# One shared table set for exponentials and logarithms, a first-block activation rounded straight from PSUM, and zero matmuls ahead of the norms

## What is computed

```
rms_norm(x, w) = x * rsqrt(mean(x*x) + 1e-6) * w
# block 1, two layers
h = rms_norm(x, pre_mix_norm[l])
proj = h @ w_in[l]            # queries, keys, values of four kinds of heads
a = neighbourhood attention; b = differential attention, then
    b = rms_norm(b, diff_subln[l]) * (1 - lambda_init)       # over 64 values of a head
c = grouped attention with normed and rotated q, k; d = latent attention
x = x + rms_norm(concat(a, b, c, d) @ w_o[l], post_mix_norm[l])
h = rms_norm(x, pre_ffn_norm[l])
x = x + rms_norm((silu(gate) * up) @ ffn_w_down[l], post_ffn_norm[l])   # gate, up = h @ ffn_w_gate_up
# block 2, four layers: mixers swa, gla, fox, swa
h = modulate(rmsnorm(x, gain), shift, scale);  x = x + g1 * mixer(h)
h = modulate(rmsnorm(x, gain), shift, scale);  x = x + g2 * swiglu(h)
# gla: log_alpha = log_sigmoid(z) / 16        fox: log_f = log_sigmoid(z + b)
```

## Time and profile before

| | |
|---|---|
| median of 3 runs | 1946.23 us (1945.25 to 1946.54) |
| the profiled execution's own time | 1951.02 us |
| its span in the trace | 1949.2 us |
| PE busy | 1883.7 us, 97% of the span, 13470 matmuls |
| PE weight loads busy | 1730.1 us, 89% |
| DVE busy | 1343.0 us, 69% |
| ACT busy | 995.4 us, 51% |
| ACT table loads in the program | 38 |
| chain that ended last, by engine | PE 81%, DVE 9%, ACT 4% of the span |

### The profile page before, as it was taken

How to read it: one execution, slowest core, us unless ns; L and a number is a source line. 1 busy time by engine, 2 the same in 40 slices (tenths; PEclk the granted TensorE clock), 3 DMA queues, 4 the chain that set the end, 5 groups by cost and what they waited for, 6 DMA issues and landing times.

```text
span 1949.2 us, 34518 instructions
## 1 busy us (share of the span) xinstructions
PE 1883.7 (97%) x13470; PEld 1730.1 (89%) x13470; DVE 1343.0 (69%) x2141; ACT 995.4 (51%) x1534; POOL 68.5 (4%) x82
## 2 busy tenths in 40 slices
PE   8999999999999999999999999998999999999998
PEld 7978999898899987899989799998989998979997
DVE  5757888675788876788878578885555555665555
ACT  7755333765533466633374453346655335655333
POOL 3002000000000000000000000003300000000000
PEclk9999999999999999999999999999999999999999
DMA  8527988532788842588853368874335554325552
GB/s 288 191 90 238 359 311 311 185 130 89 286 316 314 310 149 94 212 323 311 314 193 130 132 247 322 313 292 171 141 114 200 183 185 171 111 85 179 188 194 86
DMA packets 60355, 412.22 MB, mean 211 GB/s; under 512 B 8592, under 2 KB 8784, under 8 KB 11616
## 3 DMA queue, kind: packets, MB, share of 16 engines
q1 hardware_dynamic: 55728, 401.33, 55.7%
q0 software_dynamic: 4528, 9.56, 1.8%
HBM read 409.71 MB, written 3.16 MB: 212 GB/s over the span
## 4 chain that ended last, share of the span: by engine, by line
PE 81%; DVE 9%; ACT 4%; DVEq 2%; issue 2%; ACTq 1%; DMA 0%; SPq 0%
PE psu L502 33%; PE psy L661 16%; PE psy L564 6%; PE psy L610 5%; PE psy L556 4%; PE psm L736 3%; PE psu L519 3%; PE psu L721 2%; DVE wlo L855 2%; PE psy L632 2%; PE psy L543 1%; PE pso L707 1%; DVE ada_raw L1017 1%; DVE x L1084 1%; ACT whi L846 1%
## 5 line engine op out<-in xcount | busy, mean ns | idle before, releaser
L846 ACT CAST whi<-raw 128x2048 fp32r<-128x2048 f32 (+1 forms) x281 | 536.2, 1908 | 624.6 <-PE psu L502 424.3
L855 DVE TENSOR_TENSOR wlo<-raw,whi 128x2048 fp32r<-128x2048 f32 (+5 forms) x296 | 645.4, 2181 | 276.4 <-ACT whi L846 275.0
L502 PE MATMUL psu<-hhi,whi 128*128 128x256 f32 x1920 | 537.0, 280 | 0.0
L502 PE MATMUL psu<-hlo,whi 128*128 128x256 f32 x1920 | 535.9, 279 | 0.0
L502 PE MATMUL psu<-hhi,wlo 128*128 128x256 f32 x1920 | 535.8, 279 | 0.0
L502 PEld LDWEIGHTS psu<-hhi,whi 128*128 128x128 f32 x1920 | 360.8, 188 | 3.0
L502 PEld LDWEIGHTS psu<-hlo,whi 128*128 128x128 f32 x1920 | 360.8, 188 | 2.4
L502 PEld LDWEIGHTS psu<-hhi,wlo 128*128 128x128 f32 x1920 | 360.8, 188 | 0.0
L1017 DVE CUSTOM_DVE_ANT_0 ada_raw<-ada_raw,cvec 128x1024 f32<-128x1024 f32 x192 | 227.0, 1219 | 1.3 <-DMA ada_raw<-ada 1.2
L661 PE MATMUL psy<-whi,ahi 128*128 128x512 f32 x528 | 210.5, 399 | 1.0 <-DVE alo L1036 0.9
L661 PE MATMUL psy<-wlo,ahi 128*128 128x512 f32 x528 | 208.0, 394 | 0.0
(11 more groups left out here) (342 smaller groups left out, 3055.2 us busy)
## 6 DMA issues: line engine op xcount, KB each, us to landing
raw<-wts SPq DMA_DIRECT2D x280, 1024.0 KB, 4.8
ada_raw<-ada SPq DMA_DIRECT2D x96, 1024.0 KB, 4.8
dense_bias<-rel_bias POOLq DMA_DIRECT2D x32, 64.0 KB, 12.5
nab<-dense_bias SPq DMA_DIRECT2D x2, 1024.0 KB, 7.6
ada_raw<-fox_rows POOLq DMA_DIRECT2D x4, 512.0 KB, 6.8
cb<-cst POOLq DMA_DIRECT2D x1, 1408.0 KB, 8.5
cb<-cst SPq DMA_DIRECT2D x1, 1056.0 KB, 10.6
x<-x_in SPq DMA_DIRECT2D x2, 512.0 KB, 4.7
```

What stands on the lines that cost most here:

```text
L502: last = mm(psu[:, bank, cc * SEQ:(cc + 1) * SEQ], a[:, cols], h[:, kt, :], start=(kt == 0 and j == 0), stop=(kt == KT - 1 and j == 2))
L846: nc.scalar.copy(whi[:, part_of(c), 0:n], raw[:, slot_of(c), 0:n]).then_inc(hi_done, 1)
L855: last = nc.vector.tensor_tensor(wlo[:, part_of(c), cols], raw[:, slot_of(c), cols], whi[:, part_of(c), cols].bitcast(f32), ALU.subtract)
```

## The change

Four things are changed; the order of everything else stays.

1. In block one, `act_norm1` rounds from PSUM straight into `hhi`, two blocks at a time, and `dve_split1` takes the same PSUM value, multiplies it by the gain and subtracts `hhi`. The copy through `hw` is gone. Block two keeps the old way.
2. `pe_norm` starts 14, 14, 12, 14 and 6 zero matmuls (bf16, 128 x 512, into `psu[:, 1]`, which nothing reads) at m = 0 to 4, ahead of its wait for the first `xn_ready`.
3. In `pe_norm`, 4 blocks of the first token tile (2 at m = 0) stand ahead of the second tile's wait instead of 6, and the rest is put behind pairs of the second tile. This holds for all twelve norms.
4. `act_logs` loads a set that has both exponential and logarithm. In block one's slot 22 the root and reciprocal become exp(-0.5 ln(v)). Table loads fall from 38 to 30: by two in each layer of block one, two in gla and two in fox.

```diff
-                    pe.wait_ge(hhi_done, 8 * q + 4)
+                    pe.wait_ge(h_ready if q < 2 * DEPTH1 else hhi_done, 8 * q + 4)
...
-        def pe_norm(pe, m, q):
+        def pe_norm(pe, m, q, idle=0, ahead=4):
...
+            for _ in range(idle):
+                mm(fold(psu[:, 1], 4, P), zeros[:], zeros[:].unsqueeze(1).to_broadcast([P, 4, P]), start=True, stop=True)
             pe.wait_ge(xn_ready, NT * m + 1)
-            for kt in range(6):
+            for kt in range(ahead):
                 turned(kt, 0)
             pe.wait_ge(xn_ready, NT * m + 2)
             for kt in range(KT):
-                if kt >= 6:
-                    turned(kt, 0)
                 turned(kt, 1).then_inc(tr_done, 1)
+                if kt % 2 == 1:
+                    for k in range(ahead + kt - 1, min(ahead + kt + 1, KT)):
+                        turned(k, 0)
...
+        def act_logs():
+
+            nc.scalar.preload_act_table_set("natural_log_exp_and_others")
...
+        def act_norm1(act, q, gain, between=None):
+
+            for ks in PAIRS:
+                act.wait_ge(tr_done, 8 * q + ks[-1] + 1)
+                for k in ks:
+                    nc.scalar.activation(hhi[:, k], ps8[:, k], ACT.Identity, scale=gain[:, k:k + 1], bias=zcol[:]).then_inc(hhi_done, 1)
+                if between is not None:
+                    between(act, ks)
+
+        def dve_split1(dve, q, l, gain, between=None):
+
+            dve.wait_ge(pcol_loaded, 16 * (l + 1))
+            for ks in PAIRS:
+                dve.wait_ge(hhi_done, 8 * q + ks[-1] + 1)
+                for k in ks:
+                    nc.vector.scalar_tensor_tensor(out=hlo[:, k], in0=ps8[:, k], scalar=gain[:, k:k + 1], in1=hhi[:, k].bitcast(f32),
+                                                   op0=ALU.mult, op1=ALU.subtract).then_inc(h_ready, 1)
...
                 if h == 22:
                     act.wait_ge(sub_sum, l + 1)
-                    nc.scalar.activation(gs[:, 1, 0:8], gs[:, 0, 0:8], ACT.Sqrt, bias=epsc[:], scale=1.0 / HD).then_inc(sub_std, 1)
-                    act_table(ACT.Exp)
+                    nc.scalar.activation(gs[:, 1, 0:8], gs[:, 0, 0:8], ACT.Ln, bias=epsc[:], scale=1.0 / HD)
+                    nc.scalar.drain()
+                    nc.scalar.activation(gs[:, 2, 0:8], gs[:, 1, 0:8], ACT.Exp, scale=-0.5).then_inc(sub_std, 1)
...
                 dve.wait_ge(sub_std, l + 1)
-                nc.vector.reciprocal(gs[:, 2, 0:8], gs[:, 1, 0:8])
-                nc.vector.drain()
...
             items = heads_fox(b0)
+            act_logs()
             for h in range(FOX.slots):
...
                     nc.scalar.activation(f_l, f_l, ACT.Ln, bias=1.0).then_inc(fox_l, 1)
-                    act_table(ACT.Exp)
...
-                pe_norm(pe, 2 * l, 2 * l)
+                pe_norm(pe, 2 * l, 2 * l, 14 if l == 0 else 12, 2 if l == 0 else 4)
                 pe_mix1(pe, l)
-                pe_norm(pe, 2 * l + 1, 2 * l + 1)
+                pe_norm(pe, 2 * l + 1, 2 * l + 1, 14)
...
-                pe_norm(pe, 2 * g, 2 * g)
+                pe_norm(pe, 2 * g, 2 * g, 6 if n == 0 else 0)
```

More of the change, by code:

```diff
@@ L873, in build @@
         CHUNKS = ((0,), (1,), (2, 3), (4, 5), (6, 7))
+        PAIRS = ((0, 1), (2, 3), (4, 5), (6, 7))
         def act_sums(act, m):
@@ L893, in act_sums, with act_norm @@
                 last.then_inc(std_ready, 1)
-        def act_norm(act, q, scale, bias, between=None):
+        def act_norm1(act, q, gain, between=None):
[12 more added lines that the diff above has]
+                                                   op0=ALU.mult, op1=ALU.subtract).then_inc(h_ready, 1)
+                if between is not None:
+                    between(dve, ks)
+        def act_norm(act, q, scale, bias):
             for ks in CHUNKS:
@@ L899, in act_norm @@
                     nc.scalar.activation(hw[:, k], ps8[:, k], ACT.Identity, scale=scale[:, k:k + 1],
-                                         bias=zcol[:] if bias is None else bias[:, k:k + 1])
+                                         bias=bias[:, k:k + 1])
                 nc.scalar.drain()
                 nc.scalar.copy(hhi[:, ks[0]:ks[-1] + 1], hw[:, ks[0]:ks[-1] + 1]).then_inc(hhi_done, len(ks))
-                if between is not None:
-                    between(act, ks)
         def opening_split(act, ks):
-            if ks == (1,):
+            if ks == (0, 1):
                 act.wait_ge(raw_loaded[0], 16)
@@ L912, in opening_split, with dve_split @@
                 act_hi(act, 0, 1, first=True)
-        def dve_split(dve, q, between=None):
+        def dve_split(dve, q):
             for ks in CHUNKS:
@@ L919, in dve_split @@
                 nc.vector.tensor_tensor(hlo[:, ks_], hw[:, ks_], hhi[:, ks_].bitcast(f32), ALU.subtract).then_inc(h_ready, len(ks))
-                if between is not None:
-                    between(dve, ks)
         def opening_rest(dve, ks):
-            if ks == (1,):
+            if ks == (0, 1):
                 dve.wait_ge(hi_done, 1)
@@ L2000, in _ @@
             act.wait_ge(pcol_loaded, 16)
-            act_norm(act, 0, pcol[:, 0, 0:8], None, opening_split)
+            act_norm1(act, 0, pcol[:, 0, 0:8], opening_split)
             act_hi(act, 0, 2, first=True)
@@ L2049, in _ @@
                     dve_root_scales(dve, 2 * l, l, 1)
-                    dve_split(dve, 2 * l)
+                    dve_split1(dve, 2 * l, l, pcol[:, l, 0:8])
                     dve_lo(dve, l, 2)
@@ L2054, in _ @@
                 dve_root_scales(dve, 2 * l + 1, l, C1_FFN + 1)
-                dve_split(dve, 2 * l + 1)
+                dve_split1(dve, 2 * l + 1, l, pcol[:, l, 8:16])
                 dve_lo(dve, l, C1_FFN + 2)
```

6 lines of the change are left out of this document (3 added, 3 removed).

## The result

The changed kernel takes **1938.86 us** (median of 6 runs, 1938.36 to 1941.81) against 1946.38 us for the kernel before (6 runs): a ratio of 0.9963, 95% interval 0.9951 to 0.9974, 7.5 us less. Run again with the last experiments it took 1938.57 us, ratio 0.9962 [0.9948, 0.9975]. The forecast was 1938.2 us.

The account below looks back on a forecast made before the run. PE, busy 97% of the span, bounds the kernel, so cuts pay only where it stands still or runs slowly. Terms 1.6 + 2.1 + 1.2 + 1.5 + 1.0 + 1.3 - 0.7 = 8.0 us give 1938.2 us, range 1933.5 to 1943.

Parts of the forecast that it names:

- the four norms: Norms m = 1 to 4: zeros keep PE at 2.4 GHz and the split shortens waits; gains 1.6, 2.1, 1.2 and 1.5 us.
- the six others: Norms m = 5, 6, 7, 9, 10 and 11: ACT's first block comes earlier, 0.17 us each, 1.0 together.
- fox: Fewer table loads ahead of rounding unit 3 in fox remove PE's whole pause there: gain 1.3 us.
- the opening: Norm m = 0: slow zeros delay the transposes; loss 0.7 us, bounds from loss 1.5 to gain 1.6.
- the order at m = 8: Norm m = 8: the second identity comes late, early blocks are done anyway, so the new order changes nothing.
- gla: Table loads removed in gla: PE has no pause of note at that slot, so no gain.
- A - X: At a norm, from the second scaled identity's end (X) to ACT's first block (A); forecast 0.87 us at full clock.
- F's gain: F: moment from which PE could run without a pause; forecast earlier by 1.6, 2.1 and 1.2 us at m = 1 to 3.
- slot 22: Block one: 2.6 us of loads go, but the chain there is DVE's, so no gain and the pause stays as long.
- rival of all loads on the path: Every removed table load counts: eight at 1.283 us give 10.3 us instead of 1.3, time 1929; chance 0.04.
- Zeros that don't hold the clock: Rival: gains at m = 1 to 4 shrink, the opening loses 2.5; 4.2 us in all, 1942.0; chance 0.12.
- Later waits that take back: Rival: slot 22 and like pauses in swa grow by 3 to 4 us together, leaving 1942; chance 0.13.
- The overrun: Rival: zeros at the slow 0.44 us delay the transposes; 3 to 4 us slower, about 1950; chance 0.06.

Follow-up runs that it names:

- experiment 5: Changed kernel with the table loads of before put back, and slot 22's root and reciprocal again: 1939.37 us, ratio 0.9958 to the kernel before.

## Why the prediction was right, point by point

**The whole.** 8.0 us were forecast and 7.5 measured (9.1 in the second comparison). The terms, measured in the traces: the four norms 5.5 (said 6.4), the six others 0.7 to 1.0 (1.0), fox 1.4 (1.3), the opening -0.5 (-0.7), and two that I had put at nothing, the order at m = 8, 1.6, and gla, 0.3. Their sum is about 9. With 1.2 us less of slow clock behind the mixers' pause and the dip at 1715 us, 1.7, which only the profile of before has, that is the 11.9 us between the two spans. Misses of opposite sign, -0.9 and +1.9, partly hid each other. And the traces are one execution each: the medians differ by 7.5 and 9.1 us, the forecast lies between, and that it meets the first so closely is in part luck.

**The four norms.** The clock, A - X (0.81 to 0.86 for 0.87) and DVE's new form (479 ns on average over 32, said 0.48) are as said. What is too large is F's gain, by one misread duration and one delay that no row showed. *A transpose*: I took 0.094 us from 16 in a window of 1.50 us. A window also counts the instructions that only reach into it; from start to start 24 take 2.70 us (155.36 to 158.06), 0.1125 each. (The 0.18 at the slow clock was misread in the same way: there they stand 0.21 apart.) So at m = 1 and 3 the last transpose binds, at X + 2.76, where I had X + 2.48. *The pair*: at m = 2 I had the first `hlo` pair at A + 2.1. ACT's pair takes 1.02 us, DVE starts only at A + 1.51, and PE at A + 2.54. That is not the price of a hand-over from ACT to DVE, which is 0.10 to 0.12 us at m = 0, 1 and 3: it is the 0.39 us of unknown cause at this one place (experiment 5). Without it, in the kernel with the old tables, PE starts at A + 2.14 and F is X + 3.01, as forecast.

**The opening.** The spacing, not the clock column, told the zeros' speed, as I chose: they took 0.43 each until 11.1 us and ended at 12.27 (12.2 said), and A was 13.42 (13.4). The column read 1.00 throughout. The Trainium skill, "TensorE: Matmul & The Clock Gate", section "What's actually happening", has the throttled state as the default; the trace agrees, in 0.43 a zero against 0.22 at m = 1. The loss is -0.5 in this profile; F in four others of the changed opening, from 15.5 to 16.7, gives +0.2 to -0.9. What I did not see is that without these zeros the opening would have *gained* 2.4 (F 13.3 against 15.8).

**Fox and the tables.** Right in size and place for fox, 1.32 us, and for slot 22, nothing, where the pause only became one instead of two. The rival of all loads on the path is out by experiment 5. By the Trainium skill, "ScalarE: Activation LUTs", section "What ACT_TABLE_LOAD costs", each switch, load and drain, would be worth 2.66 us. The trace doesn't agree: the loads read 1283 ns each, and in gla of the old tables ACT needs 1.34 us from the end of the activation before the second of them (1003.04) to the start of the one behind it (1004.38). Nor was even that paid in full: three loads in fox made one pause of 1.32 us, ahead of which PE waited for DVE, and gla, which I had put at nothing, gave 0.3 us.

**Nothing at m = 8.** This step failed. I judged the order by when ACT's first block comes, which does not change there. What changes is where PE's idle time lies, 0.88 + 0.99 us or 0.43 + 0.98, and the clock answered to that. Two profiles against twelve speak for it; no run turned the order at m = 8 alone, so the cause is inferred.

**The rivals.** Zeros that don't hold the clock: out. Later waits that take back: the pause in slot 22 did not grow (3.2 and 3.25 us). The overrun: zeros at the opening run at 0.43 us, as that rival feared, but in the gaps of m = 1 to 4 at 0.22.

## What to carry to other kernels

Where the busiest engine pauses, look at the clock behind the pause and not only at the pause: in the trace of the kernel before, 17.7 us of slow clock stood behind pauses. Zero matmuls took away the 12.6 us of them behind the four norms and the mixers' pause, without making a pause shorter. The other 5.1, at 759, 1329 and 1715 us, are gone from the later traces though no zeros stand there; for the one at 1329 us the new order is the likely cause, and the other two come and go from one execution to the next. Put them into every pause of this kind that the trace shows a dip behind, close up to the awaited instruction, and not in front of a load that the real work also waits for, with the clock still low. And take a duration from start to start of a long run, never from the count in a short window.

## What the runs showed of the hardware that was not expected

- At the start the clock column reads 1.00 while matmuls run at half speed: 0.43 us a zero from 7.26 to about 11.1 us. Spacing is the thing to read there.
- How long the slow start lasts differs from one execution to the next: fourteen zeros took 4.3, 4.6, 4.9, 5.0, 5.4, 5.8 and 5.9 us in seven profiles.
- Twelve zeros, then 1.80 and 0.77 us without work, gave transposes at a clock of 0.50 for 5.9 us; seventeen zeros with pauses of 0.99 and 0.40 gave 1.00. In the first of these two profiles, running matmuls and stopping was worse than not running them; each is one execution.
- The same pause may or may not be followed by a dip: the 1.9 us wait in the first swa mixer was in the changed kernel (728 us) and not with the old tables. Two short pauses of 0.45 and 0.87 us stand ahead of the dips at 759 and 1715 us in the kernel before; the changed kernel has the same two pauses at 752 and 754 us and at 1702 and 1704, and no dip behind them. And a dip behind the same 3.2 us pause cost between 1.7 and 3.4 us.
